# A third of the expert-value sum on VectorE in the latents' two tiles of layer 0, as already in the context's two

## The reference, cut to what matters

```
def peer(h, wq, subkeys, u_tab, v_tab):
    q = (h @ wq).reshape(T, PEER_HEADS, 2, PEER_DK // 2)
    s = jnp.einsum('thcd,hcnd->thcn', q, subkeys)
    sv, si = lax.top_k(s, PEER_TOPK)
    ...                                   # 16 best sums of 16 x 16 pairs -> idx, softmax -> g
    def block(args):                      # a block of 128 tokens
        act = jax.nn.gelu(jnp.einsum('thkd,td->thk', u_tab[ib], hb))
        return jnp.einsum('thk,thkd->td', (gb * act), v_tab[ib])
```

## Time and profile before

| | us |
|---|---|
| three runs, median (lowest to highest) | 3684.89 (3677.29 to 3708.21) |
| the profiled execution, its own time | 3690.08 |
| its span in the trace | 3688.2 |
| busy: PE, DVE, POOL, ACT | 2947.4, 1958.9, 1711.3, 832.1 |
| mean granted clock of TensorE | 0.92 of full speed |

### The profile page before, as it was taken

How to read it: one execution, slowest core, us unless ns; L and a number is a source line. 1 busy time by engine, 2 the same in 40 slices (tenths; PEclk the granted TensorE clock), 3 DMA queues, 4 the chain that set the end, 5 groups by cost and what they waited for, 6 DMA issues and landing times. The chain is left out here.

```text
span 3688.2 us, 32744 instructions
## 1 busy us (share of the span) xinstructions
PE 2947.4 (80%) x10431; PEld 1726.3 (47%) x10431; DVE 1958.9 (53%) x4950; ACT 832.1 (23%) x1912; POOL 1711.3 (46%) x1540
## 2 busy tenths in 40 slices
PE   4978887868978997777897787878889668877777
PEld 2645666635445664334452232366666534322223
DVE  0213341388785676766556776213435366666662
ACT  1113321123221221212222222112332112222221
POOL 0000000147564676777777777600000177777775
PEclk7988998979889998888999999989998889999999
DMA  6764223579888999999999999933211499999997
GB/s 232 261 213 164 70 68 100 176 234 341 300 305 306 391 397 341 361 349 391 369 362 384 380 363 396 342 102 101 80 63 41 132 353 397 383 377 385 388 383 288
DMA packets 417155, 1020.60 MB, mean 277 GB/s; under 512 B 30674, under 2 KB 199898, under 8 KB 416346
## 3 DMA queue, kind: packets, MB, share of 16 engines
q0 software_dynamic: 221184, 805.40, 57.9%
q1 hardware_dynamic: 195762, 213.10, 17.9%
q10 hardware_dynamic: 40, 0.01, 0.0%
HBM read 1015.25 MB, written 3.15 MB: 276 GB/s over the span
## 5 line engine op out<-in xcount | busy, mean ns | idle before, releaser
L1755 PE MATMUL ps<-v_rows,diag 128*128 128x512 f32 x2752 | 1376.0, 631 | 383.8 <-DMA v_rows<-in_peer_v,chosen 370.3
L1687 POOL DMA_INDIRECT u_rows<-in_peer_u,chosen x768 | 846.9, 1103 | 1651.9 <-DVE chosen L1965 1224.2
L1858 DVE CUSTOM_DVE_ANT_0 u_rows<-u_rows,h_rows 128x1024 f32<-128x1024 f32 x768 | 934.2, 1220 | 468.1 <-DMA u_rows<-in_peer_u,chosen 427.9
L1755 PEld LDWEIGHTS ps<-v_rows,diag 128*128 128x128 f32 x2752 | 502.4, 197 | 1110.4 <-DMA v_rows<-in_peer_v,chosen 692.4
L1694 POOL DMA_INDIRECT v_rows<-in_peer_v,chosen x768 | 864.2, 1125 | 302.3 <-issue 159.6
L1459 PE MATMUL ps<-arena 128*128 128x256 f32 x1536 | 374.2, 400 | 37.7 <-DMA arena<-in_w_in 37.6
L1818 ACT ACTIVATE diag<-squares,coef 128x128 f32<-128x128 f32 x688 | 254.4, 397 | 635.4 <-PE ps L1755 454.2
L1459 PEld LDWEIGHTS ps<-arena 128*128 128x128 f32 x1536 | 306.1, 202 | 108.3 <-issue 56.1
L580 PE MATMUL ps<-arena 128*128 128x256 f32 (+1 forms) x896 | 211.5, 394 | 45.5 <-DMA gbias<-in_ml_gate_b 45.3
L580 PEld LDWEIGHTS ps<-arena 128*128 128x128 f32 (+1 forms) x896 | 169.6, 192 | 86.6 <-issue 56.7
L1725 PE MATMUL ps<-h,wq 128*128 128x256 f32 x768 | 194.1, 402 | 20.1 <-DMA wq<-in_peer_wq 13.4
(11 more groups left out here) (289 smaller groups left out, 2772.3 us busy)
## 6 DMA issues: line engine op xcount, KB each, us to landing
arena<-in_w_in SPq DMA_DIRECT2D x78, 1024.0 KB, 6.6
arena<-in_ada_w SPq DMA_DIRECT2D x40, 1024.0 KB, 5.5
wq<-in_peer_wq SPq DMA_DIRECT2D x48, 512.0 KB, 12.0
arena<-in_w_branch SPq DMA_DIRECT2D x24, 512.0 KB, 4.0
arena<-in_w_out SPq DMA_DIRECT2D x12, 1024.0 KB, 6.9
u_rows<-in_peer_u,chosen POOLq DMA_INDIRECT x768, 6.6
v_rows<-in_peer_v,chosen POOLq DMA_INDIRECT x768, 6.6
ada_w<-in_ada_w SPq DMA_DIRECT2D x4, 2048.0 KB, 18.1
```

The source lines that it names most:

```text
L1687: nc.gpsimd.indirect_dma_start(x.us[:, n % self.RU, :], None, self.u_rows, bass.IndirectOffsetOnAxis(x.chosen[:, w, q:q + 1], 0)).then_inc ...
L1755: ins = nc.tensor.matmul(m.ps[:, half, :], x.dg[:, (self.nth[v] - 1) % self.DIAG, :], x.vs[:, v % self.RV, half * BANK:(half + 1) * BANK], ...
L1858: nc.vector.tensor_tensor_reduce(u, u, x.ht, 1.0, 0.0, ALU.mult, ALU.add, x.dots[:, at:at + 1]).then_inc(self.u_dotted, 1)
```

## The change

The last argument of layer 0's `Peer` goes from 2 to 4 tiles. The same third of the v rows is then summed by VectorE in the latents' tiles 2 and 3: another 80 rows. Layer 1 stays without.

```
@@ -2158,7 +2158,7 @@
         norm2c = Norm(nc, sems, m, mod, 3 * KD, 0, h2, cut(arena, 2304, T), 7)
-        peer = Peer(nc, sems, m, mod, d, l, [0, CTX], h2, x, (2, 3), [], 2)
+        peer = Peer(nc, sems, m, mod, d, l, [0, CTX], h2, x, (2, 3), [], 4)
         norm = Norm(nc, sems, m, mod, 0, CTX, f.h, cut(arena, 2048, T), 6)
```

## The result

The changed kernel takes 3720.51 us in the median of four runs (3717.02 to 3730.26) against 3681.61 us of the kernel before beside it (3677.29 to 3708.21). The ratio is 1.0107, with a 95% interval from 1.0072 to 1.0142: about 1% or 39 us slower, where I had forecast 3682 us and a range up to 3708 us.

What follows compares the result with a forecast made beforehand. The prediction took the DMA transfers as the bound. Its terms, -8 (end of tile 3), -3 (dry spots), +5 and +3 (VectorE's load), summed to -3 us: 3682 us from a median of 3684.89 us, range 3663 to 3708 us.

Steps and rivals of the forecast that it cites:

- The transfers are the bound.: Latents' tiles 2 and 3, 1710 to 2355 us: DMA transfers set the pace, at shares of 0.99 to 1.00.
- What hides it is its idle time of 176.9 us: Tiles 2 and 3: VectorE's added 104 us fit into its idle time ahead of the dot products.
- The terms +5 and +3 us: Cost of VectorE's added load and waits: +5 us from 1960 to 2190 us, +3 us from 2190 to 2355 us.
- The end of tile 3, -8 us: Last v gathers of tile 3, bound by TensorE, come closer once VectorE takes 7 of 23 rows: -8 us.
- The dry spots, -3 us: Tiles 2 and 3, where TensorE's queue blocks gathers until the DMA engines run dry: less v work gains 3 us.
- C: VectorE's queue becomes the bound from 1960 us: 3703 us, chance 0.13; spread over all 645 us: 3758 us, chance 0.06.
- A: The forecast, 3682 us: transfers bind throughout, small gain at the end, small loss under VectorE's load; chance 0.66.
- B: Gathers run without gaps in all 645 us as TensorE no longer holds v buffers: 3652 us, chance 0.09.
- D: TensorE's clock stays at 1.2 GHz into the end of tile 3: +16 instead of -8, 3706 us, chance 0.06.

Runs made afterwards that it cites:

- experiment 11: Kernel before with h in PSUM in layer 1, plus every third of the last 18 v rows given to VectorE in both layers: 3657.15 us, ratio 0.9930.
- the first experiment: Changed kernel with the latents' 78 two-operand VectorE sums replaced by one-operand TENSOR_REDUCEs of the same v rows: 3687.92 us, ratio 1.0009.

## Why the prediction was wrong

**The step that failed is the first, "The transfers are the bound."** GpSimd's queue bound as well, and in tile 3 it was full. The row from 2190 us in the earlier trace rows shows it: 119 gathers, 127.74 us busy, and 0.30 us ahead of each make 163 of 165 us. I had read only GpSimd's waits, and taken 0.99 and 1.00 of DMA share for the limit, with the 1.03 of another stretch in the same table. The 4.3 us of waits for VectorE were no measure of what VectorE costs GpSimd: 77 us of held time in the same 645 us were inside its busy time. Divided by the count, that row gives 1.07 us a gather; the last one in the earlier trace rows took 0.94 us. This difference was the question to ask.

**"What hides it is its idle time of 176.9 us"** The earlier trace rows failed with it. VectorE's load was costed well (104 us of instructions; its stretches are at 68%, 79% and 65%, for 72%, 87% and 77% forecast, as the stretches got longer). It was not VectorE's time that ran out: its two-operand instructions took time from another engine. The terms +5 and +3 us of the sum, all that the prediction had for VectorE's work, so measured +54 us of held time and +7 us of waits for VectorE, less 15 us of waits for TensorE: the stage's 46 us. That choosing ended at 2295 us and not at 2277 us, on which the +3 leaned, matters little beside this.

**The end of tile 3, -8 us**, came to -1. The prediction had misread the rows: from 2356.82 to 2391.71 us there are 20 intervals of 1.74 us, not 19 of 1.84, and two of the gathers waited for nothing; its own way of counting then gives -7. As measured, the last u gather began at 2405.43 us and the last v gather at 2440.53 us, 35.1 us; before, 2355.58 to 2391.71 us, 36.1 us. TensorE was no longer busy throughout (25 of 36 us), yet the gathers came hardly closer, and experiment 11 found no more. A v buffer is free only after landing and sum, and there are five: one turn of 5 x 1.8 = 9 us is near to a gather's way to its landing (6.5 us in the median of the page) and a sum. That is argued; no run has more buffers.

**The dry spots, -3 us**: GpSimd's waits for TensorE fell from 42.4 to 11.5 us as forecast (below 15). What the dry spots alone gave can't be told from the trace; the relief is small beside the rest.

**The rivals.** The outcome lies between C's two forms, but C's mechanism isn't what happened: dot products came late 8 times, 15 us in all, within what A had named, while C stood for over 50 us. VectorE's queue was never the bound. B is out. D came half true: the clock fell to 0.80 from 2225 us on, as the earlier trace rows let expect; it stood at 0.95 at the end of tile 3, and the first experiment has the same clock without the loss. The rule of the Trainium skill named there, from its page "TensorE: Matmul & The Clock Gate" (short runs of matmuls between waits for transfers let the clock fall), agrees with the trace, and it had no price here.

The rule that did apply I had not weighed: the Trainium skill, page "SBUF — State Buffer", section "Who interferes with whom", says that a VectorE instruction with two SBUF inputs contends with a GpSimd instruction that reads SBUF. The traces agree: gathers of up to 2.05 us, rarely more, against 0.94 us, and none held with one operand in PSUM. The same section infers that such instructions leave descriptor generation alone; these indirect gathers, which read their row numbers from SBUF, are held all the same. Which part of a gather it is that stands, its reading or its generating, no run here separates.

## What to carry to other kernels

Divide an engine's busy time by its instruction count and compare with its shortest instance. Waits inside an instruction are counted as work, and an engine whose busy time plus issue pauses fills the stretch is a bound, whatever the DMA share says. Before moving work to an engine with idle time, ask what its instructions hold up for others. In a kernel that lives on GpSimd's gathers, a VectorE instruction with two large SBUF operands can have a second price, as long as GpSimd's queue is full, and one operand in PSUM removes it. Here that was worth 1% (3649 us against 3685 us), more than any shift of work between the engines.

## What was unexpected about the hardware

- An indirect gather on GpSimd takes 0.94 us, or, begun within a VectorE instruction that reads two SBUF operands (1.22 to 1.28 us long), until 0.81 us after that instruction's end, up to 2.05 us. Two of 1536 gathers took longer in the kernel before and two after, up to 3.40 us; why is open. Begun within a TENSOR_REDUCE of the same length it took 0.94 us (59, 63 and 70 gathers in three kernels), as did one begun within the same dot product with one operand in PSUM (223 gathers).
- The DMA engines moved 382 GB/s at a shown share of 1.00 and 408 GB/s at 1.03 with the same gathers. A share of 1.00 was no limit; whether 1.03 is one is argued from three kernels that end there.
- What VectorE does in front of a two-operand instruction changes how long that one holds a gather: 80 us rose to 92 us by 74 reduces that hold nothing themselves (one execution each; 75 to 81 us in those with the code of before).
